# Another order of the tensors in SBUF: rounded weights, h and y at chosen addresses

## The reference

```
h = rms_norm(x, norm_pre_w)
proj = h @ w_in          # q,k,v,z of mixer A; beta, decay; q,k,v,z of mixer B; two gates
A: causal conv (4 taps) + SiLU on q,k,v; q,k l2-normalised; chunked gated delta rule, 8 heads of 128
   ya = rms_norm(oa, dn_onorm_w) * silu(z_a)
B: softmax attention, 8 heads of 128, causal, with a relative-position bias
   yb = ob * silu(z_b)
merged = sigmoid(g0 + b0) * (ya @ w_branch[0]) + sigmoid(g1 + b1) * (yb @ w_branch[1])
out = x + rms_norm(merged @ w_out, norm_post_w)
```

## Time and profile before

| | us |
|---|---|
| median of 3 runs (357.30 to 357.66) | 357.52 |
| the profiled execution | 357.55 |
| its span, first to last instruction | 355.8 |
| TensorE busy in it | 347.6 |

### The profile page before, as it was taken

One profiled execution on the slowest core, in us unless ns is written; L12 is line 12 of the kernel. 1 busy time (PEld: TensorE's weight loads), 2 busy tenths in 40 slices (PEclk: granted clock), 3 DMA queues, 4 the chain that ended last, 5 costly groups with the idle time before them and its releaser, 6 DMA issues.

```text
span 355.8 us, 6674 instructions
## 1 busy us (share of the span) xinstructions
PE 347.6 (98%) x2387; PEld 318.4 (89%) x2387; DVE 270.0 (76%) x551; ACT 218.8 (62%) x483; POOL 58.7 (16%) x114
## 2 busy tenths in 40 slices
PE   7999999999999999999999999999999999999993
PEld 5889998888899999999999999999998888888882
DVE  3869897599997868978788797878977656566744
ACT  5877894542457667686867766777676544425421
POOL 1534436500050000301103020030301101000011
PEclk9999999999999999999999999999999999999999
DMA  8667948793698485446745565465534735766423
GB/s 264 178 193 194 334 158 270 198 329 119 167 257 228 121 214 141 121 122 164 188 120 128 145 178 147 120 164 145 165 121 138 247 118 172 254 226 236 124 113 118
DMA packets 76206, 63.48 MB, mean 178 GB/s; under 512 B 4724, under 2 KB 62478, under 8 KB 76174
## 3 DMA queue, kind: packets, MB, share of 16 engines
q1 hardware_dynamic: 73838, 59.37, 57.3%
q0 software_dynamic: 1152, 3.30, 3.1%
q10 hardware_dynamic: 1184, 0.39, 0.5%
HBM read 61.46 MB, written 1.59 MB: 177 GB/s over the span
## 4 chain that ended last, share of the span: by engine, by line
PE 84%; DVE 8%; DMA 3%; issue 2%; ACT 1%; POOL 0%; DVEq 0%; SPq 0%; ACTq 0%; POOLq 0%
PE banks L1395 40%; PE banks L1450 15%; PE banks L1657 6%; PE banks L1413 6%; DVE w_lo L919 3%; DVE sub L1061 2%; DMA xin<-in_x_dram 1%; DMA raw<-in_w_in_dram 1%; DMA sub<-m_blocks 1%; PE banks L1545 1%; PE banks L1523 1%; PE banks L1562 1%; PE banks L1551 1%; PE banks L1380 1%; DVE sub L1063 1%
## 5 line engine op out<-in xcount | busy, mean ns | idle before, releaser
L919 DVE TENSOR_TENSOR w_lo<-raw,w_hi 128x1024 fp32r<-128x1024 f32 x102 | 123.8, 1220 | 42.3 <-ACT w_hi L670 41.6
L670 ACT CAST w_hi<-raw 128x1024 fp32r<-128x1024 f32 x103 | 107.2, 1047 | 30.0 <-PE banks L1450 12.3
L1395 PE MATMUL banks<-h_hi,w_hi 128*128 128x256 f32 x440 | 64.0, 288 | 0.2 <-DVE acc L989 0.2
L1395 PE MATMUL banks<-h_lo,w_hi 128*128 128x256 f32 x440 | 59.4, 277 | 0.0
L1395 PE MATMUL banks<-h_hi,w_lo 128*128 128x256 f32 x440 | 59.3, 277 | 0.0
L1395 PEld LDWEIGHTS banks<-h_hi,w_hi 128*128 128x128 f32 x440 | 55.2, 189 | 0.7 <-DVE acc L989 0.3
L1395 PEld LDWEIGHTS banks<-h_hi,w_lo 128*128 128x128 f32 x440 | 54.2, 188 | 0.0
L1395 PEld LDWEIGHTS banks<-h_lo,w_hi 128*128 128x128 f32 x440 | 54.2, 188 | 0.0
L989 DVE SCALAR_TENSOR_TENSOR acc<-banks,vec,acc 128x255 f32<-128x255 f32 (+2 forms) x72 | 34.5, 480 | 3.7 <-ACT acc L790 1.5
L616 POOL TENSOR_TENSOR so<-so,rnq 128x2 f32<-128x2 f32 x8 | 2.0, 251 | 162.8 <-ACT junk L857 162.8
L790 ACT ACTIVATE acc<-banks,vec 128x256 f32<-128x256 f32 x16 | 7.6, 473 | 17.4 <-PE banks L1395 17.4
(11 more groups left out here) (258 smaller groups left out, 607.6 us busy)
## 6 DMA issues: line engine op xcount, KB each, us to landing
raw<-in_w_in_dram SPq DMA_DIRECT2D x80, 512.0 KB, 4.9
raw<-in_w_branch_dram SPq DMA_DIRECT2D x16, 512.0 KB, 4.7
raw<-in_w_out_dram SPq DMA_DIRECT2D x8, 512.0 KB, 4.2
xin<-in_x_dram SPq DMA_DIRECT2D x2, 512.0 KB, 3.8
th_E<-g_rows POOLq DMA_DIRECT2D x2, 512.0 KB, 7.2
bias<-bias_rows POOLq DMA_DIRECT2D x1, 1024.0 KB, 7.5
raw<-in_x_dram SPq DMA_DIRECT2D x2, 512.0 KB, 3.7
out_dram<-xin SPq DMA_DIRECT2D x4, 256.0 KB, 2.0
```

Source lines behind the costliest of these rows:

```text
L670: nc.scalar.copy(w_hi[:, t % SLOTS, :], raw[:, t % SLOTS, :]).then_inc(s_hi, 1)
L919: v.tensor_tensor(w_lo[:, t % SLOTS, cols], raw[:, t % SLOTS, cols], w_hi[:, t % SLOTS, cols].bitcast(F32), ALU.subtract).then_inc(s_lo, 1)
L1395: last = mm(ps, w, r, start=part == 0 and k == 0, stop=part == 2 and k == KT - 1)
```

## The change

Only the order of the `sb` calls changes. Eleven tensors are allocated earlier than before; no size, no type, no instruction and no wait is touched.

```diff
+        gt = sb("gt", [P, 12, NC, HEADS])
+        wbd2 = sb("wbd2", [P, KT, 4 * HEADS], F32R)
+        ssqk = sb("ssqk", [P, NC, HEADS])
+        ng = sb("ng", [P, NC, HEADS])
         raw = sb("raw", [P, SLOTS, D])
         w_hi = sb("w_hi", [P, SLOTS, D], F32R)
         w_lo = sb("w_lo", [P, SLOTS, D], F32R)
+        bd = sb("bd", [P, NC, 2 * HEADS])
+        alog = sb("alog", [P, HEADS])
+        dtb = sb("dtb", [P, HEADS])
+        h_hi = sb("h_hi", [P, KT, SEQ], F32R)
+        h_lo = sb("h_lo", [P, KT, SEQ], F32R)
+        y_hi = sb("y_hi", [P, 2, HEADS, SEQ], F32R)
+        y_lo = sb("y_lo", [P, 2, HEADS, SEQ], F32R)
         xin = sb("xin", [P, NC, D])
...
         wbd = sb("wbd", [P, KT, 2 * HEADS])
-        wbd2 = sb("wbd2", [P, KT, 4 * HEADS], F32R)
         bd_lo = sb("bd_lo", [P, NC, 2 * HEADS])
-        alog = sb("alog", [P, HEADS])
-        dtb = sb("dtb", [P, HEADS])
-        h_hi = sb("h_hi", [P, KT, SEQ], F32R)
-        h_lo = sb("h_lo", [P, KT, SEQ], F32R)
         bias = sb("bias", [P, HEADS, SEQ])
         tiny = sb("tiny", [P, 32])
-        bd = sb("bd", [P, NC, 2 * HEADS])
-        gt = sb("gt", [P, 12, NC, HEADS])
         tab = sb("tab", [P, 11, HEADS])
-        ng = sb("ng", [P, NC, HEADS])
         grow = sb("grow", [HEADS, SEQ])
-        ssqk = sb("ssqk", [P, NC, HEADS])
...
         y32 = sb("y32", [P, 2, SEQ])
-        y_hi = sb("y_hi", [P, 2, HEADS, SEQ], F32R)
-        y_lo = sb("y_lo", [P, 2, HEADS, SEQ], F32R)
```

## The result

The changed kernel is slower by a little: 359.52 us (median of 4 runs, 359.33 to 360.06) against 357.54 us for the kernel before on the same chip, a ratio of 1.0059 with a 95% interval of 1.0041 to 1.0076. Its profiled execution took 359.60 us with a span of 357.8, 2.0 us more than before. No instruction differs.

The account below looks back on a forecast made before the run. The prediction took TensorE's matmul rate before 60 us and after 104 us to bound the kernel. Its terms summed to 0 on the profiled execution, forecasting 357.5 us, own range 356.8 to 358.2, whole range 351 to 362.

Parts of the forecast that it names:

- What bounds the kernel: How fast TensorE gets through its matmuls before 60 us and after 104 us sets the end; TensorE is 84% of the span.
- the one on the tensors from acc to y32: These tensors keep their place mod 2048, so the float32 matmuls on them see nothing: no cost.
- rival B: The slow phase becomes the rule: all line 1395 tiles take 2.83 for 2.74 us, +4.1, so 361.6 us; chance 0.18.
- the term of the slow tiles: Line 1395's tiles at the slower rate cost about 0.6 us in all; change taken as 0, at best -0.6 us.
- Moving operand w: 0: Lines 1413, 1450 and 1657, weight h or y: 229.5 ns a matmul stays, at most 14.5 ns lost to placement; taken as 0.
- the step that the distance above 256 has no price: Pieces with h and y as weight take the same though their distances from w differ by 256 bytes: below 0.1 ns each.
- The main reason for 0: Line 1395 against the lines with w moving: 0.446 and 0.448 ns a column at two places, so placement costs 0.
- The phase "follows from when a block begins": Weight and column streams lock in one of two phases by when a block begins; it could fall otherwise, -0.6 us at best.
- VectorE and ScalarE: 0: w_lo's subtractions and ScalarE's copy cost the same at both places: 0, bound 0.1 us either way.
- Transfers, 0 to -0.7 us: Loads into raw at a rounder start: only one raw wait, at 94.92 us, is on the chain, so 0 to -0.7 us.
- the median landing of w_in, named as its sign: Landings of w_in under 4.9 us, with a shorter wait at 95 us, would show that transfers gain.
- Rival A: Aligned streams are faster: lines 1413, 1450 and 1657 give -6.0 us, 351.5; with line 1395 too 345.3; chance 0.20.

Follow-up runs that it names:

- b_wh: The kernel before with unused bytes that move only w, h and y to the changed kernel's places: 358.23 us, ratio 1.0004.
- b_c: The kernel before with only xin and the constants (cst) moved by 64 bytes: 358.62 us, ratio 1.0019.
- b_dup: The kernel before with one transpose of head 0 issued twice, no address changed: 357.91 us, ratio 1.0006.
- a_dup: The changed kernel with one transpose of head 0 issued twice, no address changed: 359.48 us, ratio 1.0037 to the kernel before.
- b_shift: The kernel before with 128 unused bytes ahead of all its tensors, every distance kept: 357.34 us, ratio 0.9986.
- a_shift: The changed kernel with 128 unused bytes ahead of all its tensors, every distance kept: 359.72 us, ratio 1.0058 to the kernel before.
- b_whc: The kernel before with w, h, y, xin and cst all moved to the changed kernel's places by unused bytes: 359.61 us, ratio 1.0041.
- b_shift2: The kernel before with 128 unused bytes ahead of all its tensors, measured again on another chip: 357.20 us, ratio 0.9984.

## Why the prediction was wrong

**What bounds the kernel**: right. The end is set by TensorE's rates, and one of them moved.

**The step that failed** is the one on the tensors from acc to y32: "so the float32 matmuls on kT_all, act, T_all, sc and pt see nothing", with rival B's "the distance mod 256 between the two streams is kept". Both are true of those matmuls and of the pair w and h. What changed was a third distance, from w and h to what TensorE read just before: T_all and act lay 128 from h and now lie 0 from it; cst lay 0 from w and now lies 192 from it, and 0 from h. The list of places in the prediction holds all of them, and none of these differences was taken. b_wh and b_c price them: 8 more slow tiles from w and h, 6 from cst, 22 from both. In the sum it is the term of the slow tiles that failed: 0, at best -0.6 us, where it measured +2.0.

**Moving operand w: 0**: right, 229 ns stayed, and so did the step that the distance above 256 has no price: y went from 448 to 192 mod 512 and its pieces from 20.15 to 20.14 us.

**The main reason for 0**, that 0.446 and 0.448 ns a column at two places mean a rate that doesn't care for the place, was no evidence. Both cases had w and h 192 apart; distance was the one thing that the earlier trace rows did not vary. It costs up to 1.9% of the kernel's time when it does.

**The phase "follows from when a block begins"**: wrong for the 22 tiles, right for single ones. b_dup and a_dup move every later start and leave the pattern from the third head on, b_shift and a_shift move the places and leave it; b_whc makes it by distances. In head 0 of b_dup a pause of 0.09 us went with the other rate. The two rates are real, and what picks one in the later heads is how far w and h lie from the other tensors. The own range of 356.8 to 358.2 fell with this.

**VectorE and ScalarE: 0**: right, 1218 ns for w_lo against 1.22 us.

**Transfers, 0 to -0.7 us**: right in kind, -0.4 in b_shift, though the median landing of w_in, named as its sign, is still 4.9 us there (4.8 in b_shift2). In the change it is not to be had: after and a_shift differ in raw's place as before and b_shift do, and take 359.52 and 359.72 us. Slow matmuls between 97 and 106 us are in its stead; chain after, then b_shift:

```profile
97.44 8.48 PE banks L1395 x72
```

```profile
97.32 8.18 PE banks L1396 x72
```

118 ns a matmul against 114, so TensorE itself is not free until 105.92 us in the changed kernel and is at 105.50 in b_shift.

**Rival A**: wrong as a mechanism. Runs that begin at 0 gained nothing for the streams; the best that any placement gave 512 columns was 227 ns, 1%, where it had 6.3%, and that by distance.

**Rival B**: the right line, the right price (0.09 us a tile, 2.83 for 2.74), the wrong extent: 24 of 44 tiles, so 359.5 instead of 361.6. Its point from which it decides, one tile in six, was passed; a chance of 0.18 was too low for a rate that the trace already showed on the same line, for a reason that I had only argued.

## What to carry to other kernels

When tensors move, list the place modulo 256 of everything that TensorE reads, and compare differences, not places: between the two operands of a matmul, and between them and the operands of the matmul ahead. If a trace shows one instruction on the same addresses at two rates, a placement change can reprice it over its whole count; give that a large chance and count the pieces at each rate. To try a placement, shift by unused bytes first: one pad ahead of everything keeps the distances and gives the transfers their start (0.4 us here), and any other pad changes distances.

## What the runs showed of the hardware

- TensorE's float32r rate depends on the distance mod 256 bytes from w to h or y, its two operands: 114 to 120 ns for 256 columns, 227 to 233 ns for 512, at the granted clock of 1.00 in these stretches. The lines with 256 columns, w loaded, are fastest at 192, those with 512, w streaming, at 0.
- At 192 there are two rates for 256 columns, 114 and 118 ns. From the third head on the distances from w and h to what the mixers' matmuls and transposes read choose between them (2, 8, 10 or 24 slow tiles of 44); in the first head a pause of 0.09 us went with a change as well. What collides stays open.
- The Trainium skill, page "SBUF — State Buffer", section "Who interferes with whom", has TensorE reading weights and moving operand over two independent ports and never waiting on anyone. The prediction took from it that placement costs nothing. The measurement decides: the same instruction costs up to 5% more by where its own two operands lie.
- Transfers of the same bytes take 2% less queue time into tiles that begin at 0 mod 256 than into ones at 128.
